# Transformer block pair on one core: order of turns, splits and copies in the attention stage, and the bank of the last chunk

## The chip, the core and the metric

The kernel runs on one core of a Trainium2 chip. Its engines are TensorE (PE, matrix products and transpositions), VectorE (DVE), ScalarE (ACT), GpSimd (POOL) and SyncE (SP); each works through its own program in order and waits on semaphores. The metric is the time of one execution on the device, in microseconds (us); lower is better. The time before is 1011.17 us, the median of three runs.

## The reference, cut to what matters

The input is 256 tokens of width 1024. A first block of two layers comes first; then the second block, whose attention is the third stage that is changed here:

```python
hn = rms_norm_2(x, ln_g[l])
proj = jnp.einsum('bsd,dc->bsc', hn, w_in[l])
(qa, ka, va, ga, qb, kb, vb, gb, qc, kc, vc, gc, gate_logits) = jnp.split(proj, SPLIT_POINTS, axis=-1)
o_a = moba_attention(...)        # 8 heads of 64
o_b = dilated_attention(...)     # 3 x 8 heads of 64
o_c = swa_sink_attention(...)    # 8 heads of 64, keys and values of only 2 shared heads
branches = jnp.stack([o_a * silu(ga), o_b * silu(gb), o_c * silu(gc)], axis=2)
br = jnp.einsum('bsiw,iwd->bsid', branches, w_branch[l])
merged = jnp.sum(sigmoid(gate_logits) * br, axis=2)
x = x + jnp.einsum('bsd,de->bse', merged, w_out[l])
```

Queries and keys are normalised per head before the logits; the logits get a bias by distance, then a softmax.

## The kernel before, in words

**Weights and matmuls.** The 256 tokens are two blocks of 128. Weights come from memory in units of at most 2048 columns per partition (1 MB) into a ring of three slots. ACT rounds a unit to `w_hi` (`round_unit`, L1022), DVE takes the rest `w_lo` (`split_unit`, L1662), and PE makes three matmuls in place of one, `hi*hi`, `hi*lo` and `lo*hi` (L434 to L436). SP loads the next unit into a slot when the slot's split is done (L262). ACT and DVE work two units ahead of PE: `slot_step` (L1034, L1669) rounds or splits the unit that PE needs two steps later. A step is one unit of four 128-row pieces on both blocks, 24 matmuls; a chunk of up to 512 output columns is two steps, and goes to the banks `acc[0]` and `acc[1]`, one for each block.

**The five attention groups.** The heads of the third stage run in five groups of eight heads, as four pairs each. The first three are passes of a loop (full attention and two dilations), the fourth is the third dilation, the fifth the window with shared keys. While a group's attention runs, PE also projects the next three chunks, so a group is six steps s = 0 to 5. In PE's program (`project_and_attend`, L661 to L689), for pair t:

- turns (`turn_pair`, L567; `turn_tokens`, L573): four transpositions of queries and keys into one bank, `qkT_ps`, which is `acc[2]`; pair 0 in the middle of step 0 (between the two blocks), pair 1 before step 1, pair 2 in its middle, pair 3 at its end. Each waits until ACT has copied the pair before out of the bank;
- logits of pair s at the end of step s, then the turn of the probabilities of pair s-1 (`turn_probs`, L600), then the values of pair s-2 (`values`, L620);
- turn of the outputs of pair s-3 (`turn_outputs`, L635) in the middle of steps 3, 4 and 5, and of pair 3 after step 5. It waits until ACT has copied these outputs and until DVE has read those of the pair before out of the bank.

ACT (`project_and_attend`, L1183) does in a step, in this order: copy of outputs, `slot_step`, what is left of the chunk before, copies of turned pairs (`copy_pair`, L1121, two activations each), the exponentials of pair s-1 and the copy of the probabilities of pair s-2, at step 1 the copy of pair 3, and then the copy of a chunk that has ended. DVE (L1910) does `slot_step`, the maxima of pair s (`maxima`, L1750), its half of the copy of probabilities, the reading of outputs (`token_outputs`, L1817) and the group's own extras. A step number in `late` moves `slot_step` behind the step's attention work; on DVE it still stands ahead of the reading of outputs. Before, `late` is (4,) in the fourth group and empty in the others.

**Between the fourth and the fifth group.** The last chunk of the fourth group is 256 wide: keys and values of the two shared window heads. ACT copies and squares it (`window_kv`, L1477); DVE sums the squares (L2155), makes the scale and writes the scaled keys to all eight heads in two instructions, one for each block (`window_keys`, L2150, L2161). The second of them releases the first turn of the fifth group through `qk_ready`.

**The end.** Six gate chunks and six branch chunks alternate in `acc[0:2]`; ACT copies the last one to `branch_out` (L1640). PE then waits for all reads, `pe.wait_ge(acc_read, n.chunk * 2)`, and starts the output projection, which uses all four `acc` banks.

Of the kernel before, what the change touches and what calls it, by code (L numbers as in the profile page):

```python
# [24 lines left out]
P = 128  # L25
TB = 2
# [44 lines left out]
def build_program(nc, x, w_in0, w_uq, w_ukv, w_out0, w_qkv, rel_band, w_out1, w_gate, w_up, w_down, g_final,  # L71
# [7 lines left out]
    with ctx:  # L79
# [85 lines left out]
        qk_banks = [qkT_ps[:, :]] + acc_banks  # L165
# [5 lines left out]
        def probs_of(kind, t):  # L171
            return mla_probs[t] if kind == "mla" else logit[:, t % 3, :, :]

# [31 lines left out]
        qk_ready = sem("qk_ready")  # L205
        qkT_done = sem("qkT_done")
# [205 lines left out]
        def _(pe):  # L412
# [154 lines left out]
            def turn_pair(kind, t, banks=(0,)):  # L567

                qkT_ps = qk_banks[banks[t % len(banks)]]
                since(pe, qkT_read, n.turn - min(t, len(banks) - 1))  # L570
                turn_tokens(t, qkT_ps)

# [88 lines left out]
            def project_and_attend(widths, kind, qk, copied, outs=head_outs, closing=None):  # L661
# [5 lines left out]
                for width in widths:  # L667
                    for k0 in (0, 4):
                        def between(blk, s=s):
                            if s == 0 and blk == 1:  # L670
                                group_ready(qk, copied)
                                pe.wait_ge(out_read, pair0)
                                turn_pair(kind, 0)
                            if s == 1:
                                turn_pair(kind, 1 + blk)
                            if s >= 3 and blk == 1:
                                turn_outputs(s - 3, pair0, turn0, outs)
                            if s == 5 and blk == 1:
                                if closing:
                                    closing()  # L680
                                attention_step(kind, 5, pair0, turn0)
                        chunk_unit(uT_hi, uT_lo, range(k0, k0 + 4), width, k0 == 0, k0 == 4, between)
                        if s == 1:
                            turn_pair(kind, 3)
                        if s < 5:
                            attention_step(kind, s, pair0, turn0)
                        s += 1
# [288 lines left out]
            for i in range(3):  # L976
                if i:
                    turn_branch(i, turn_banks)
                for half in range(2):
# [6 lines left out]
                    chunk(oT_hi, oT_lo, 4, 512, x_kt=4 * (i % 2))  # L986
# [15 lines left out]
        def _(act):  # L1002
# [118 lines left out]
            def copy_pair(kind, t, pair0, banks=(0,)):  # L1121

                qkT_ps = qk_banks[banks[t % len(banks)]]
                act.wait_ge(qkT_done, n.turn + 1)
                if kind == "last":
                    activation(qkT[:, t, 0:S], qkT_ps[:, 0:S], ACT.Copy, scale=g_now[:, 0:1])
                    activation(qkT[:, t, S:2 * S], qkT_ps[:, S:2 * S], ACT.Copy,
                               scale=g_now[:, 1:2]).then_inc(qkT_read, 1)
                else:
                    activation(qkT[:, t, :], qkT_ps[:, :], ACT.Copy).then_inc(qkT_read, 1)  # L1130
# [1203 lines left out]
```

## Time and profile before

| | |
|---|---|
| time, median of 3 runs (lowest to highest) | 1011.17 us (1009.79 to 1012.47) |
| time of the profiled execution | 1009.69 us |
| its span, first to last instruction | 1007.9 us |
| PE busy | 984.0 us, 98% |
| DVE busy | 629.4 us, 62% |
| ACT busy | 594.7 us, 59% |
| DMA | 170.26 MB, 169 GB/s over the span |
| mean granted clock of TensorE | 0.998 |

Busy is the time in which at least one instruction of the engine was in work. Rows of the timeline give start, duration, engine, line, operation, target <- sources, shapes and count, and in brackets the idle time before and what ended it. Matmuls overlap, so their pace is read from the distance of starts and not from their durations.

### The profile page before, as it was taken

Reading aid. Unit: us, or ns where it says so; the run is one execution under the profiler, and the core shown is the slowest. Engines: PE = TensorE matmul, PEld = TensorE weight load, DVE = VectorE, ACT = ScalarE, POOL = GpSimd, SP = SyncE. Lnnn points to the kernel's source line nnn. Section 1 sums busy time; section 2 is a strip of 40 time slices with the busy share of each in tenths; the row PEclk is TensorE's granted clock in tenths of the full one; section 3 lists DMA queues with packets and bytes.
Section 4 is the critical chain, followed back from the end, with each engine's and each line's share of the span. In section 5 each row is a group of like instructions: output and inputs, shape, how many; then the busy total and the mean of one; then the engine's idle time right before and its main releaser. Section 6 shows DMA issues by size and latency. Waiting matters only on the chain.

```text
span 1007.9 us, 13330 instructions
## 1 busy us (share of the span) xinstructions
PE 984.0 (98%) x4920; PEld 791.8 (79%) x4920; DVE 629.4 (62%) x782; ACT 594.7 (59%) x929; POOL 12.2 (1%) x22
## 2 busy tenths in 40 slices
PE   6999899999999999999999999999999998999998
PEld 5888688888887777788888887877777777778877
DVE  5676675555556765665555556866666666776654
ACT  6776564444445655465454545766767676867571
POOL 1000000000000000000000000000000000000000
PEclk9999999999999999999999999999999999999999
DMA  8536247756563543457757654646434334336551
GB/s 272 177 114 204 84 137 239 247 169 206 168 206 128 180 155 125 127 168 254 227 188 227 231 185 132 207 163 199 132 125 134 116 126 135 118 124 209 197 179 42
DMA packets 106041, 170.26 MB, mean 169 GB/s; under 512 B 3988, under 2 KB 65302, under 8 KB 106000
## 3 DMA queue, kind: packets, MB, share of 16 engines
q1 hardware_dynamic: 103360, 161.23, 48.6%
q0 software_dynamic: 2304, 8.37, 2.6%
q8 instruction: 27, 0.44, 0.2%
q10 hardware_dynamic: 336, 0.10, 0.0%
q14 instruction: 14, 0.11, 0.0%
HBM read 168.58 MB, written 1.11 MB: 168 GB/s over the span
## 4 chain that ended last, share of the span: by engine, by line
PE 91%; ACT 4%; DVE 4%; issue 1%; DMA 0%; ACTq 0%; DVEq 0%
PE acc L434 13%; PE acc L436 12%; PE acc L435 12%; PE acc L485 11%; PE pair_ps L436 7%; PE pair_ps L434 7%; PE pair_ps L435 7%; PE acc L536 3%; PE acc L713 3%; PE acc L630 2%; PE turn_ps L609 2%; PE pair_ps L597 1%; PE acc L577 1%; PE pair_ps L596 1%; PE turn_ps L503 1%
## 5 line engine op out<-in xcount | busy, mean ns | idle before, releaser
L1666 DVE TENSOR_TENSOR w_lo<-w_raw,w_hi 128x2048 fp32r<-128x2048 f32 (+2 forms) x155 | 345.5, 2231 | 133.4 <-ACT w_hi L1027 133.0
L1027 ACT ACTIVATE w_hi<-w_raw 128x2048 fp32r<-128x2048 f32 (+2 forms) x155 | 288.4, 1863 | 78.3 <-PE acc L436 35.5
L434 PE MATMUL acc<-w_hi,uT_hi 128*128 128x512 f32 (+3 forms) x552 | 221.4, 401 | 3.5 <-DVE w_lo L2093 3.0
L436 PE MATMUL acc<-w_hi,uT_lo 128*128 128x512 f32 (+3 forms) x552 | 212.5, 385 | 0.0
L435 PE MATMUL acc<-w_lo,uT_hi 128*128 128x512 f32 (+3 forms) x552 | 211.9, 384 | 0.0
L434 PEld LDWEIGHTS acc<-w_hi,uT_hi 128*128 128x128 f32 x552 | 104.0, 188 | 30.9 <-issue 9.0
L434 PE MATMUL pair_ps<-w_hi,uT_hi 128*128 128x512 f32 x320 | 126.5, 395 | 0.0
L436 PE MATMUL pair_ps<-w_hi,uT_lo 128*128 128x512 f32 x320 | 124.8, 390 | 0.0
L435 PE MATMUL pair_ps<-w_lo,uT_hi 128*128 128x512 f32 x320 | 124.6, 389 | 0.0
L436 PEld LDWEIGHTS acc<-w_hi,uT_lo 128*128 128x128 f32 x552 | 104.0, 188 | 21.2
L435 PEld LDWEIGHTS acc<-w_lo,uT_hi 128*128 128x128 f32 x552 | 104.3, 189 | 17.4
L436 PEld LDWEIGHTS pair_ps<-w_hi,uT_lo 128*128 128x128 f32 x320 | 60.0, 188 | 12.8
L435 PEld LDWEIGHTS pair_ps<-w_lo,uT_hi 128*128 128x128 f32 x320 | 60.2, 188 | 12.0
L434 PEld LDWEIGHTS pair_ps<-w_hi,uT_hi 128*128 128x128 f32 x320 | 60.1, 188 | 11.9
L1150 ACT ACTIVATE logit<-logit,negmax 128x128 f32<-128x128 f32 (+1 forms) x124 | 54.7, 445 | 13.7 <-DVE negmax L1763 13.7
L1509 ACT ACTIVATE oT_hi<-turn_ps 128x512 fp32r<-128x512 f32 x22 | 13.2, 599 | 76.1 <-PE turn_ps L503 76.1
L1758 DVE SCALAR_TENSOR_TENSOR logit<-pair_ps,bias 128x256 f32<-128x256 f32 (+1 forms) x56 | 28.6, 552 | 44.6 <-PE pair_ps L597 43.6
L485 PE MATMUL acc<-w_hi,oT_hi 128*128 128x512 f32 x176 | 54.4, 390 | 0.7 <-ACT logit L1109 0.7
L2053 DVE SCALAR_TENSOR_TENSOR qkv<-pair_ps,norms,qkv 128x256 f32<-128x256 f32 x40 | 17.5, 479 | 59.8 <-ACT qkv L1505 59.8
L485 PE MATMUL acc<-w_lo,oT_hi 128*128 128x512 f32 x176 | 54.2, 389 | 0.0
L485 PE MATMUL acc<-w_hi,oT_lo 128*128 128x512 f32 x176 | 54.2, 389 | 0.0
L1109 ACT ACTIVATE qkv<-acc,norms 128x512 f32<-128x512 f32 x44 | 29.6, 685 | 36.1 <-PE acc L436 36.1
(230 smaller groups left out, 1230.9 us busy)
## 6 DMA issues: line engine op xcount, KB each, us to landing
w_raw<-in_w_in SPq DMA_DIRECT2D x46, 1024.0 KB
w_raw<-in_w_gate SPq DMA_DIRECT2D x44, 512.0 KB
w_raw<-in_w_up SPq DMA_DIRECT2D x44, 512.0 KB
w_raw<-in_w_down SPq DMA_DIRECT2D x22, 1024.0 KB
w_raw<-in_w_out SPq DMA_DIRECT2D x12, 1024.0 KB
w_raw<-in_w_qkv SPq DMA_DIRECT2D x16, 512.0 KB
w_raw<-in_w_branch SPq DMA_DIRECT2D x6, 1024.0 KB
bias<-rel_rows POOLq DMA_DIRECT2D x5, 1024.0 KB, 7.9
```

The costliest lines, as they stand in the source:

```text
L434: mm(o, xh, wh[:, k, :], start=first and k == 0, stop=False)
L435: mm(o, xh, wl[:, k, :], start=False, stop=False)
L436: done = mm(o, xl, wh[:, k, :], start=False, stop=last and k == len(kts) - 1)
L485: done = mm(acc[2 * blk + half][:, :], xp, wp[:, k, 512 * half:512 * half + 512], start=first and k == 0 and i == 0, stop=last and k == 1 ...
L536: done = mm(acc[2 * blk + half][:, :], xp, wp[:, k, 512 * half:512 * half + 512], start=False, stop=k == 1 and j == 2)
L609: done = transpose(turn_ps[:, j, P * i:P * i + P], probs_of(kind, t)[:, j, P * i:P * i + P], ident[:, :])
L713: done = mm(acc[2 * blk + half][:, :], xp, wp[:, k, 512 * half:512 * half + 512], start=first and k == 0 and j == 0, stop=last and k == 1 ...
L1027: activation(w_hi[:, slot, 0:width], w_raw[:, slot, 0:width], ACT.Copy).then_inc(hi_done, 1)
L1109: done = activation(dst, src, func, scale=scale)
L1150: done = activation(pr[:, j, cols], pr[:, j, cols], ACT.Exp, bias=negmax8[:, blk, head], accum_out=total8[:, blk, head])
L1666: v.tensor_tensor(w_lo[:, slot, 0:width], w_raw[:, slot, 0:width], w_hi[:, slot, 0:width].bitcast(f32), ALU.subtract).then_inc(lo_done, 1)
L1758: done = v.scalar_tensor_tensor(pr[:, :, cols][:, :, ::-1], pair_ps[:, :, cols][:, :, ::-1], scale, bias_of(t, mask_cols), ALU.mult, ALU.add)
```

## The change

It has five parts. (1) In a group, PE turns the pairs 0, 1 and 2 in one go in the middle of step 0, into three banks (`qkT_ps` and the two halves of `turn_ps`), and pair 3 at the end of step 0, behind a wait for the copy of pair 0. ACT copies pairs 0, 1, 2 in step 0 and pair 3 in step 1 ahead of the exponentials. Before the logits of step 1 PE waits until three pairs are copied. (2) The turns of the outputs of pairs 0 and 1 move from the middle of steps 3 and 4 to their ends, behind the values; that of pair 2 moves behind the values in the middle of step 5. (3) `late` becomes (4, 5) in the fourth group and (2,) in the fifth, and DVE's reading of outputs comes before a late `slot_step`. (4) The window keys are written in three pieces, the first for the first pair alone, both blocks at once; it releases the first turn, and a new semaphore, `keys_spread`, releases the turns of pairs 1 and 2, which in this group follow step 0. (5) The last branch chunk goes to `acc[2:4]`.

```diff
-        qk_banks = [qkT_ps[:, :]] + acc_banks
+        qk_banks = [qkT_ps[:, :]] + turn_banks + [qkT_ps[:, :]]
...
+        def branch_banks(i, half):
+            return acc[2:4] if (i, half) == (2, 1) else acc[0:2]
...
-            def turn_pair(kind, t, banks=(0,)):
-
-                qkT_ps = qk_banks[banks[t % len(banks)]]
-                since(pe, qkT_read, n.turn - min(t, len(banks) - 1))
-                turn_tokens(t, qkT_ps)
...
                             if s == 0 and blk == 1:
                                 group_ready(qk, copied)
                                 pe.wait_ge(out_read, pair0)
-                                turn_pair(kind, 0)
-                            if s == 1:
-                                turn_pair(kind, 1 + blk)
-                            if s >= 3 and blk == 1:
-                                turn_outputs(s - 3, pair0, turn0, outs)
+                                for t in range(1 if n.window else 3):
+                                    turn_tokens(t, qk_banks[t])
                             if s == 5 and blk == 1:
                                 if closing:
                                     closing()
                                 attention_step(kind, 5, pair0, turn0)
+                                turn_outputs(2, pair0, turn0, outs)
                         chunk_unit(uT_hi, uT_lo, range(k0, k0 + 4), width, k0 == 0, k0 == 4, between)
+                        if s == 0 and n.window:
+                            pe.wait_ge(keys_spread, 1)
+                            for t in (1, 2):
+                                turn_tokens(t, qk_banks[t])
+                        if s == 0:
+                            pe.wait_ge(qkT_read, turn0 + 1)
+                            turn_tokens(3, qk_banks[3])
                         if s == 1:
-                            turn_pair(kind, 3)
+                            pe.wait_ge(qkT_read, turn0 + 3)
                         if s < 5:
                             attention_step(kind, s, pair0, turn0)
+                        if s in (3, 4):
+                            turn_outputs(s - 3, pair0, turn0, outs)
...
-                    chunk(oT_hi, oT_lo, 4, 512, x_kt=4 * (i % 2))
+                    chunk(oT_hi, oT_lo, 4, 512, x_kt=4 * (i % 2), banks=branch_banks(i, half))
...
-                    for t in ((0,), (1, 2))[s] if s < 2 else ():
-                        copy_pair(kind, t, pair0)
+                    for t in ((0, 1, 2), (3,))[s] if s < 2 else ():
+                        copy_pair(t)
                     attention_step(kind, s, pair0, head0)
                     if s in late:
                         slot_step(prefetch[s])
-                    if s == 1:
-                        copy_pair(kind, 3, pair0)
...
-                               prefetch=(UNIT, UNIT, 1024, 1024, UNIT, UNIT), late=(4,))
+                               prefetch=(UNIT, UNIT, 1024, 1024, UNIT, UNIT), late=(4, 5))
             project_and_attend([swish_gate(1), swish_gate(2), lambda: gate_exponentials(0)], "last", 32, 8, outs=window_outs,
-                               after={3: factors(0, 1, 4), 5: lambda: split_banks(oT_hi, 0, 4, pair_banks)})
+                               after={3: factors(0, 1, 4), 5: lambda: split_banks(oT_hi, 0, 4, pair_banks)}, late=(2,))
...
-                    copy_chunk(lambda blk: [(branch_out[:, blk, :], acc[blk][:, :], ACT.Copy, 1.0)])
+                    banks = branch_banks(i, half)
+                    copy_chunk(lambda blk: [(branch_out[:, blk, :], banks[blk][:, :], ACT.Copy, 1.0)])
...
                     attention_step(kind, s, n.pair, head0, bias_of)
+                    if 3 <= s:
+                        token_outputs(s - 3, n.pair, head0)
                     if s in late:
                         slot_step(prefetch[s])
-                    if 3 <= s:
-                        token_outputs(s - 3, n.pair, head0)
...
-                for blk in range(TB):
-                    done = v.tensor_tensor(
-                        qkv[:, 1, blk, :].rearrange("p (g r d) -> p g r d", g=2, r=4),
-                        window_kvs[:, blk, 0:P].rearrange("p (g d) -> p g d", g=2).unsqueeze(2).broadcast_to([P, 2, 4, HD]),
-                        stat[:, 2, 2 * blk:2 * blk + 2].unsqueeze(2).unsqueeze(3).broadcast_to([P, 2, 4, HD]), ALU.mult)
-                done.then_inc(qk_ready, 1)
+                scale = stat[:, 2, 0:4].rearrange("p (b n) -> p b n", b=TB)
+
+                def spread(group, r0, count):
+                    c0 = HD * (4 * group + r0)
+                    return v.tensor_tensor(
+                        qkv[:, 1, :, c0:c0 + HD * count].rearrange("p b (r d) -> p b r d", d=HD),
+                        window_kvs[:, :, HD * group:HD * group + HD].unsqueeze(2).broadcast_to([P, TB, count, HD]),
+                        scale[:, :, group:group + 1].unsqueeze(3).broadcast_to([P, TB, count, HD]), ALU.mult)
+                spread(0, 0, 2).then_inc(qk_ready, 1)
+                spread(0, 2, 2)
+                spread(1, 0, 4).then_inc(keys_spread, 1)
```

DVE's two calls get the same `late` as ACT's.

## Rows read from the trace of the kernel before

**Rows 1.** The page: busy time of each engine, and what the DMA moved.

```profile
PE 984.0 (98%) x4920; PEld 791.8 (79%) x4920; DVE 629.4 (62%) x782; ACT 594.7 (59%) x929; POOL 12.2 (1%) x22
...
DMA packets 106041, 170.26 MB, mean 169 GB/s; under 512 B 3988, under 2 KB 65302, under 8 KB 106000
```

**Rows 2.** Waits, PE: us in total, times, longest.

```profile
PE acc L434 <- DVE w_lo L2093: 3.0, 1, 3.0
...
PE acc L485 <- ACT logit L1109: 0.7, 1, 0.7
```

**Rows 3.** Timeline, PE, end of the fourth group and first half of the fifth.

```profile
835.71 0.28 PE L436 MATMUL acc<-w_hi,uT_lo 128*128 128x256 f32 x1
837.17 0.41 PE L641 MATMUL acc<-ident,heads 128*128 128x128 f32 x2 [1.18 <-issue]
...
842.61 0.39 PE L436 MATMUL acc<-w_hi,uT_lo 128*128 128x512 f32 x1
844.11 0.66 PE L577 MATMUL acc<-ident,qkv 128*128 128x128 f32 x4 [1.12 <-DVE qkv L2161]
...
856.18 0.88 PE L609 MATMUL turn_ps<-ident,logit 128*128 128x128 f32 x6
857.56 0.47 PE L434 MATMUL acc<-w_hi,uT_hi 128*128 128x512 f32 x1 [0.51 <-ACT bias L1109]
...
864.79 0.84 PE L609 MATMUL turn_ps<-ident,logit 128*128 128x128 f32 x6 [0.66 <-ACT logit L1150]
```

**Rows 4.** Timeline, PE, first pass of the loop: four turns, then six, between matmuls.

```profile
660.27 0.60 PE L577 MATMUL acc<-ident,qkv 128*128 128x128 f32 x4
...
660.93 0.40 PE L435 MATMUL acc<-w_lo,uT_hi 128*128 128x512 f32 x1
661.17 0.40 PE L436 MATMUL acc<-w_hi,uT_lo 128*128 128x512 f32 x1
...
672.29 0.88 PE L609 MATMUL turn_ps<-ident,logit 128*128 128x128 f32 x6
673.01 0.50 PE L434 MATMUL acc<-w_hi,uT_hi 128*128 128x512 f32 x1
```

**Rows 5.** Timeline, DVE, end of the fourth group: splits, readings of outputs, window keys.

```profile
834.44 2.29 DVE L1666 TENSOR_TENSOR w_lo<-w_raw,w_hi 128x2048 fp32r<-128x2048 f32 x1 [0.29 <-ACT w_hi L1027]
836.65 0.42 DVE L1821 TENSOR_SCALAR heads<-acc 128x256 f32<-128x256 f32 x1
836.99 2.28 DVE L1666 TENSOR_TENSOR w_lo<-w_raw,w_hi 128x2048 fp32r<-128x2048 f32 x1
...
840.26 0.42 DVE L1821 TENSOR_SCALAR heads<-acc 128x256 f32<-128x256 f32 x1 [0.66 <-PE acc L641]
...
841.08 0.42 DVE L2155 TENSOR_REDUCE stat<-square 128x4 f32<-128x256 f32 x1 [0.24 <-ACT square L1484]
...
842.76 1.29 DVE L2161 TENSOR_TENSOR qkv<-bias,stat 128x512 f32<-128x512 f32 x2
```

**Rows 6.** Timeline, ACT, both groups: probabilities, pair 3, rounding, exponentials.

```profile
836.49 0.48 ACT L1156 ACTIVATE prT<-turn_ps 128x384 f32<-128x384 f32 x1
...
855.42 0.47 ACT L1126 ACTIVATE qkT<-acc,g_now 128x256 f32<-128x256 f32 x1 [0.62 <-PE acc L577]
...
860.67 1.90 ACT L1027 ACTIVATE w_hi<-w_raw 128x2048 fp32r<-128x2048 f32 x1
862.47 0.39 ACT L1150 ACTIVATE logit<-logit,negmax 128x128 f32<-128x128 f32 x1
```

**Rows 7.** Windows: eight turns in a row of the fifth group; PEclk is the granted clock.

```profile
core 0: us, PE busy (x) PEld busy (x) DVE busy (x) ACT busy (x) POOL busy (x), PEclk, DMA share, GB/s
885.20:886.30 1.10, 1.10 (x13) 0.93 (x12) 1.07 (x2) 0.40 (x1) 0.00 (x0) 1.00 0.00 0
```

**Rows 8.** Waits of SP's DMA queue, 800 to 930 us: total, times, longest.

```profile
SPq L266 <- DVE w_lo L1666: 121.6, 18, 12.9
```

**Rows 9.** Timeline, PE, start of the program: first and last of six such matmuls.

```profile
11.71 0.63 PE L435 MATMUL acc<-w_lo,uT_hi 128*128 128x512 f32 x1
...
13.84 0.63 PE L434 MATMUL acc<-w_hi,uT_hi 128*128 128x512 f32 x1
```

More of the change, by code:

```diff
@@ L205, in build_program @@
         qk_ready = sem("qk_ready")
+        keys_spread = sem("keys_spread")
         qkT_done = sem("qkT_done")
@@ L1118, in plain, with copy_pair @@
                 return lambda blk: [(dst(blk), banks[blk][:, 0:width], ACT.Copy, scale_of(blk))]
-            def copy_pair(kind, t, pair0, banks=(0,)):
-                qkT_ps = qk_banks[banks[t % len(banks)]]
+            def copy_pair(t):
+                bank = qk_banks[t]
                 act.wait_ge(qkT_done, n.turn + 1)
[L1125 to L1130, printed above, removed]
+                activation(qkT[:, t, 0:S], bank[:, 0:S], ACT.Copy, scale=g_now[:, 0:1])
+                activation(qkT[:, t, S:2 * S], bank[:, S:2 * S], ACT.Copy,
+                           scale=g_now[:, 1:2]).then_inc(qkT_read, 1)
                 n.turn = n.turn + 1
@@ L2159, in window_keys @@
                 sharpen(*[stat[:, i, 0:4] for i in range(4)], HD)
-                for blk in range(TB):
-                    done = v.tensor_tensor(
-                        qkv[:, 1, blk, :].rearrange("p (g r d) -> p g r d", g=2, r=4),
-                        window_kvs[:, blk, 0:P].rearrange("p (g d) -> p g d", g=2).unsqueeze(2).broadcast_to([P, 2, 4, HD]),
-                        stat[:, 2, 2 * blk:2 * blk + 2].unsqueeze(2).unsqueeze(3).broadcast_to([P, 2, 4, HD]), ALU.mult)
-                done.then_inc(qk_ready, 1)
+                scale = stat[:, 2, 0:4].rearrange("p (b n) -> p b n", b=TB)
[8 more added lines that the diff above has]
+                spread(1, 0, 4).then_inc(keys_spread, 1)
                 n.qk = n.qk + 1
             project_and_attend(6, "last", 24, table(3), {1: head_sums, 3: lambda: swish_gate(0), 5: window_keys},
-                               prefetch=(UNIT, UNIT, 1024, 1024, UNIT, UNIT), after_unit={2: head_norm(0)}, late=(4,))
+                               prefetch=(UNIT, UNIT, 1024, 1024, UNIT, UNIT), after_unit={2: head_norm(0)}, late=(4, 5))
             def nm(group):
@@ L2241, in _ @@
                 0: full_over_total, 1: lambda: swish_gate(1), 2: first_gate, 3: lambda: swish_gate(2),
-                4: dilation_weights}, closing={5: lambda: split_banks(oT_hi, oT_lo, 0, 4, pair_banks)})
+                4: dilation_weights}, closing={5: lambda: split_banks(oT_hi, oT_lo, 0, 4, pair_banks)}, late=(2,))
             for i in range(3):
```

## The prediction

> **What bounds the kernel now.** I read the page first. The matrix engine (PE) has work in flight for 98% of the span [rows 1], so only its idle time and its time per instruction can give anything. The list of waits comes next. Its PE part is short, and its largest entry, 3.0 us, lies at the start of the program, outside the change [rows 2]. Then I went through PE's timeline over the five attention groups of the third stage. In the three groups of the loop no gap is listed. The gaps lie in the last two groups [rows 3]:
>
> - fourth group, middle of step 5: the stream stops after the matmul at 835.71, and the next instruction, the turn of the outputs of pair 2, starts at 837.17. Without a wait it would start about 0.12 later (a 256-wide matmul's pace, half of the 0.23 that a 512-wide one takes [rows 4]), so 1.34 us are lost.
> - fifth group, first turn of pair 0: 842.61 to 844.11, 1.27 us lost beyond one matmul.
> - fifth group, start of the second chunk: 856.18 to 857.56, for six turns that take 0.11 each [rows 4]: 1.38 - 0.66 = 0.72 lost.
> - fifth group, probabilities of pair 1: 0.66 idle, put down to ACT's exponentials.
>
> Who releases them is read from the other two engines. The first gap is called "issue", but the turn waits until DVE has read the outputs of pair 1 (836.65), and DVE does that only after a split of weights begun at 834.44 and 2.29 long [rows 5]. Right behind it the values of pair 3 would wait anyway: ACT copies their probabilities at 836.49, behind a rounding of weights [rows 6]. The second gap ends with DVE's two instructions from 842.76, which write the window keys to all heads. They end a chain whose sum starts at 841.08, after the reading of pair 3's outputs at 840.26 [rows 5]. The third ends with ACT's copies of the chunk, which stand behind the copy of pair 3 at 855.42; the fourth with exponentials at 862.47, which stand behind the rounding at 860.67 [rows 6].
>
> **The change, part by part.** Times are in us; gains are negative.
>
> *Turns in one go.* Four turns take 0.43: from 660.27 to the second matmul behind them at 660.93 is 0.66, less one matmul of 0.23 (660.93 to 661.17 is 0.24) [rows 4]. Twelve in a row then take 1.3, as three times four do now. Entering and leaving the turns shows no price of its own in these rows, so the move costs 0. The nearest rows bound it at 0.1 either way per group, five groups: -0.5 to +0.5. The same holds for the turns of outputs that move behind the values. What hides the copies: pair 0 must be read by ACT (two copies of 0.47 [rows 6]) while PE runs the second half of step 0, 12 matmuls of 0.23 or 2.7. Pairs 1 and 2 have all of step 1, 24 matmuls or 5.5. If that cover were gone, PE would pay up to 0.85 per pair. Logits of pair 0 come 1.3 later in the step (12 turns stand in front of them, none today), and DVE's maxima and ACT's exponentials of pair 0 move with them. They are needed only behind step 1.
>
> *Clock.* Eight turns in a row ran at a granted clock of 1.00, the 2.4 GHz level [rows 7]. The Trainium skill (TensorE: Matmul & The Clock Gate, Part 4: PE-mode transpose) says that turns on this engine do not count as busy time for its clock; by that rule the longer run of turns could let the clock fall, and the sum would lose some 6 us. By the row it loses 0, which I take.
>
> *Copy of pair 3 first.* It leaves the place between the exponentials and the chunk's copies, so ACT reads the chunk as soon as PE ends it. Fifth group: -0.72. In the loop the same spot shows 672.29 to 673.01 for six turns, 0.72 against 0.66 or less [rows 4]; I take -0.1 for each of four groups, -0.4 (between 0 and -0.7). What is late next there: nothing that I find before the end of the chunk.
>
> *Split of step 2 behind the exponentials, fifth group.* The rounding at 860.67 takes 1.90 [rows 6] and stands in front of exponentials for which PE waits 0.66 [rows 3]. With the two exchanged, and the chunk's copies earlier as well, the gap closes: -0.66 (bounds 0 and -0.66). The rounding and DVE's split come some 4 later. PE needs that unit two steps on, over 10 away; were that cover gone, PE would wait for what is missing.
>
> *Outputs before splits, fourth group.* DVE reads pair 1's outputs before the split of 2.29, and ACT copies pair 3's probabilities before the rounding of 1.91: both releasers of the first gap come forward by over 1.3, and the gap closes: -1.34. What is queued behind: DVE's split of step 4 now waits for PE's turn and for that read, 0.42, so it ends about 837.2. The read of pair 2 follows at 837.2, and the split of step 5, which began at 836.99 [rows 5], now begins about 837.5 and ends 839.8. Pair 3's outputs, turned by PE at about 838.5, are read only then, at 839.7, not 840.26, and the sum of the keys starts at about 840.25, not 841.08: 0.83 earlier, though PE is 1.34 earlier.
>
> *Keys as a piece.* The two instructions from 842.76 take 1.29 for 1024 elements per partition [rows 5]. The first piece has 256. A DVE read of 256 elements takes 0.42 (836.65) [rows 5]; a quarter of 1.29 would be 0.32, one of today's two 0.65. I take 0.42, by the row of its own size: 0.87 earlier. The first turn then starts at 844.11 - 0.83 - 0.87 = 842.4, and PE reaches it at 842.84 - 1.34 = 841.5. A gap of 0.9 stays of 1.27: -0.37 (bounds: 0 with a late chain, -1.27 if it closes). The two other pieces, about 1.1 together, are done by 843.6; PE asks for them some 2.7 after the first turn.
>
> *Loads.* The splits that come later also free their slots later, by at most some 4, and SP's loads wait for exactly these splits [rows 8]. A unit of 1 MB at the mean rate of 169 GB/s [rows 1] takes about 6.2. It is rounded three steps after the split that freed the slot, some 16 or more even with short steps, so this stays hidden. GpSimd's queue has no part in these stretches.
>
> *Last chunk in other banks.* PE still waits for both reads of every chunk before the output projection, which is the 0.7 in the list [rows 2]; only the bank number changes. 0.
>
> **Sum.** 0.72 + 0.4 + 0.66 + 1.34 + 0.37 = 3.5 off. The profiled execution took 1009.69, its span 1007.9; the sum makes that 1006.2 and 1004.4. Its time is 1.5 below the median of the three runs (1011.17) and 0.1 below their fastest, so as base for the median I take the mean of all four times, 1010.8: **1007.3**.
>
> **Rivals.** A measurement of this kernel tells about 0.3% from no change, 3.0 us here: faster means below 1008.1.
>
> *The logits' delay takes the freed places.* In the fifth group the logits of pair 0 stand behind 12 turns, 1.3 later in the step; if ACT's exponentials of pair 0 then end so late that the chunk is again read late, the gaps of 0.72 and 0.66 return in another form. For it: ACT is a single queue, and each step of that chain stood in a gap today. Against it: pair 2's copy and pair 3's copy leave that very stretch. 3.5 - 1.4 = 2.1 off: 1008.7. Chance 0.22.
>
> *More closes than I count.* The remaining 0.9 at the first turn and the 0.7 ahead of the output projection (if the other banks release it after all) vanish: 5.1 off, 1005.7. Chance 0.12.
>
> *The clock falls behind the long run of turns.* At the start of the program matmuls ran at the lower level, 1.2 GHz: six records of 0.63, 0.43 apart, against 0.23 later [rows 9]. Before them PE had waited 3.0 [rows 2]. If twelve turns alone bring such a spell, each group loses at least 6 x 0.2 = 1.2; five groups 6.0, so 2.5 slower than before: 1013.3. It decides from three groups on. Against it: eight turns at 1.00 [rows 7], with matmuls directly before and behind. Chance 0.06. The page named above is the rule for this case; the trace does not bear it out for eight turns, and shows no twelve.
>
> *The change doesn't do what it says.* For the banks of the last chunk this is my forecast (0). For the rest the waits that are named do stand in the code that moves.
>
> **How the numbers follow.** Forecast 0.60, at 1007.3 with about 1 us of scatter either way, as the four times show. Of it some four fifths lie below 1008.1; with nearly all of the second rival and a quarter of the first this makes 0.63 faster. The rest of the forecast and most of the first rival make 0.29 for no difference; the clock, with a little for a wait that I have not seen, 0.08 slower. The range takes in the second rival with some scatter, and the first with more, since single runs of one kernel lie up to 2.8 apart: 1004.3 to 1010.3.
>
> **What would show it.** In the new profile: no wait in the fourth group's step 5; the first turn of the fifth group still after an idle time of about 0.9, ended by DVE's first piece; no idle time at the second chunk and none before the probabilities of pair 1 there; each pass of the loop shorter by about 0.1; the wait of 0.7 ahead of the output projection unchanged; granted clock 1.00 behind the runs of turns. Wrong would be a new wait of PE for ACT's copies behind step 0 or 1, for weights (w_lo) in steps 1 or 4 of the fifth group, or for the gated outputs that DVE splits at the end of the fifth group: its reads of outputs now wait for turns that come later in each step.

## The result and the profile after

| | before | after |
|---|---|---|
| time, median of 4 runs (lowest to highest) | 1010.48 us (1009.79 to 1012.47) | 1005.19 us (1005.08 to 1007.22) |
| time of the profiled execution | 1009.69 us | 1005.24 us |
| its span | 1007.9 us | 1003.5 us |

The ratio is 0.9947 (95% interval 0.9932 to 0.9961): faster, by 0.5%. The forecast was 1007.3 with a range of 1004.3 to 1010.3. Whole times of one kernel scatter by up to three us, in part because of a spell in the first layers that this change does not touch (last section). So from here on I compare what can be read to a hundredth: starts in PE's timeline. **The stretch** is the distance from the last weight matmul ahead of the first turns (before 660.03, after 660.30) to the last weight matmul of the program (before 1004.37, after 999.92). To the nanosecond it is 4.71 us shorter, where the prediction's sum was 3.5.

PE's line on the page, after:

```profile
PE 982.2 (98%) x4920; PEld 792.1 (79%) x4920; DVE 629.8 (63%) x783; ACT 595.1 (59%) x929; POOL 12.2 (1%) x22
```

Against [rows 1] PE's busy time fell by 1.8 us with the same 4920 instructions: part of the gain is not in any listed wait.

A pass of the loop is read from the first weight matmul behind the first turns of a pass. PE's timeline before:

```profile
707.13 0.47 PE L434 MATMUL acc<-w_hi,uT_hi 128*128 128x512 f32 x1
...
753.64 0.47 PE L434 MATMUL acc<-w_hi,uT_hi 128*128 128x512 f32 x1
```

and PE's timeline after, over the whole third stage (L438 to L440 are the three weight matmuls, L575 the turns of queries and keys, L607 those of probabilities, L628 the values, L639 the turns of outputs):

```profile
660.53 0.60 PE L575 MATMUL acc<-ident,qkv 128*128 128x128 f32 x4
...
661.76 0.48 PE L438 MATMUL acc<-w_hi,uT_hi 128*128 128x512 f32 x1
...
680.54 0.87 PE L628 MATMUL acc<-prT,qkv 128*64 128x256 f32 x8
...
681.35 0.50 PE L438 MATMUL acc<-w_hi,uT_hi 128*128 128x512 f32 x1
681.68 0.39 PE L439 MATMUL acc<-w_lo,uT_hi 128*128 128x512 f32 x1
...
688.68 0.87 PE L628 MATMUL acc<-prT,qkv 128*64 128x256 f32 x8
689.48 0.44 PE L639 MATMUL acc<-ident,heads 128*128 128x128 f32 x2
...
689.99 0.39 PE L439 MATMUL acc<-w_lo,uT_hi 128*128 128x512 f32 x1
...
707.96 0.48 PE L438 MATMUL acc<-w_hi,uT_hi 128*128 128x512 f32 x1
...
754.12 0.48 PE L438 MATMUL acc<-w_hi,uT_hi 128*128 128x512 f32 x1
...
834.69 0.28 PE L440 MATMUL acc<-w_hi,uT_lo 128*128 128x256 f32 x1
834.90 0.87 PE L628 MATMUL acc<-prT,qkv 128*64 128x256 f32 x8
...
841.36 0.66 PE L575 MATMUL acc<-ident,qkv 128*128 128x128 f32 x4 [0.80 <-DVE qkv L2165]
...
853.39 0.87 PE L607 MATMUL turn_ps<-ident,logit 128*128 128x128 f32 x6
854.02 0.47 PE L438 MATMUL acc<-w_hi,uT_hi 128*128 128x512 f32 x1
...
860.55 0.88 PE L607 MATMUL turn_ps<-ident,logit 128*128 128x128 f32 x6
...
976.29 0.39 PE L440 MATMUL acc<-w_hi,oT_lo 128*128 128x512 f32 x1
977.37 0.73 PE L489 MATMUL acc<-w_hi,oT_hi 128*128 128x512 f32 x2 [0.69 <-ACT logit L1114]
```

The reader should see four things. First, against [rows 3]: the gap in step 5 of the fourth group is gone (the values follow at 834.90 on the matmul at 834.69, with no idle time), the one at the second chunk of the fifth group is gone (six turns from 853.39 to 854.02, 0.63), the one ahead of the probabilities (860.55) is gone, and 0.80 is left at the first turn. Second, the wait ahead of the output projection is still 0.69, as in [rows 2]. Third, twelve turns in a row take 1.23 from 660.53 to the next matmul. Fourth, a pass of the loop went from 753.64 - 707.13 = 46.51 to 754.12 - 707.96 = 46.16 (46.15 unrounded), 0.35 less, though no wait was ever listed there.

Where the 4.71 us lie, each from differences of matmul starts, beside the prediction's term:

| stretch | predicted | measured |
|---|---|---|
| three passes of the loop | 0.3 | 1.01 |
| fourth group up to the middle of step 5 | 0.1 | 0.28 |
| the gap in step 5 and the rest of that step | 1.34 | 1.41 |
| first turn of the fifth group | 0.37 | 0.33 |
| fifth group, up to the probabilities of pair 1 (second chunk) | 0.72 | 0.76 |
| rest of the fifth group (exponentials, outputs) | 0.66 | 0.88 |
| behind it | 0 | 0.04 |

DVE's timeline after, at the end of the fourth group, answers to [rows 5]:

```profile
833.58 0.42 DVE L1822 TENSOR_SCALAR heads<-acc 128x256 f32<-128x256 f32 x1 [0.61 <-PE acc L639]
833.91 2.28 DVE L1667 TENSOR_TENSOR w_lo<-w_raw,w_hi 128x2048 fp32r<-128x2048 f32 x1
836.18 0.42 DVE L1822 TENSOR_SCALAR heads<-acc 128x256 f32<-128x256 f32 x1
836.52 2.28 DVE L1667 TENSOR_TENSOR w_lo<-w_raw,w_hi 128x2048 fp32r<-128x2048 f32 x1
838.72 0.42 DVE L1822 TENSOR_SCALAR heads<-acc 128x256 f32<-128x256 f32 x1
...
839.20 0.42 DVE L2156 TENSOR_REDUCE stat<-square 128x4 f32<-128x256 f32 x1
...
840.88 1.36 DVE L2165 TENSOR_TENSOR qkv<-bias,stat 128x256 f32<-128x256 f32 x3
```

From 833.58 to the sum at 839.20 DVE has not one pause: reads and splits alternate as predicted, and the first turn waits for the length of this queue. ACT's timeline after, fifth group, answers to [rows 6]:

```profile
848.49 0.49 ACT L1130 ACTIVATE qkT<-acc,g_now 128x256 f32<-128x256 f32 x1
...
850.96 0.70 ACT L1114 ACTIVATE square<-acc,norms 128x512 f32<-128x512 f32 x1
...
855.99 0.39 ACT L1152 ACTIVATE logit<-logit,negmax 128x128 f32<-128x128 f32 x1
...
858.12 1.90 ACT L1032 ACTIVATE w_hi<-w_raw 128x2048 fp32r<-128x2048 f32 x1
```

Pair 3 (848.49) now goes ahead of the chunk's copies (850.96), and the exponentials of pair 1 (855.99) go ahead of the rounding (858.12). Granted clock after, windows in the first layers and over the twelve turns (third number from the right):

```profile
115.00:118.00 3.00, 3.00 (x14) 2.21 (x16) 3.00 (x5) 0.00 (x0) 0.00 (x0) 1.00 0.94 296
...
660.50:661.80 1.30, 1.30 (x14) 1.26 (x12) 0.87 (x1) 1.02 (x3) 0.00 (x0) 1.00 0.95 369
```

So the signs that the prediction named are all there but one: each pass is shorter by 0.35, not by 0.1. What this leaves to find out is which part of the change made which of these gains.

### The profile page after: what moved, and what is told of

It reads as the page before. It is cut to its first block, busy times and chain, and to the rows that moved or that the text cites. A ratio compares the mean times of both kernels' runs of the same rounds, so it can differ in the third digit from the quotient of the medians.

```text
span 1003.5 us, 13324 instructions
## 1 busy us (share of the span) xinstructions
PE 982.2 (98%) x4920; PEld 792.1 (79%) x4920; DVE 629.8 (63%) x783; ACT 595.1 (59%) x929; POOL 12.2 (1%) x22
## 4 chain that ended last, share of the span: by engine, by line
PE 91%; DVE 4%; ACT 3%; issue 1%; DMA 0%; ACTq 0%; DVEq 0%
PE acc L438 13%; PE acc L440 12%; PE acc L439 12%; PE acc L489 11%; PE pair_ps L440 7%; PE pair_ps L438 7%; PE pair_ps L439 7%; PE acc L540 3%; PE acc L718 3%; PE turn_ps L607 2%; PE acc L628 2%; PE pair_ps L595 2%; DVE w_lo L1667 1%; PE pair_ps L594 1%; PE turn_ps L507 1%
## 5 line engine op out<-in xcount | busy, mean ns | idle before, releaser
L438 PE MATMUL acc<-w_hi,uT_hi 128*128 128x512 f32 (+3 forms) x552 | 219.6, 398 | 2.8 <-DVE w_lo L2094 2.8
L440 PE MATMUL acc<-w_hi,uT_lo 128*128 128x512 f32 (+3 forms) x552 | 212.4, 385 | 0.0
L438 PEld LDWEIGHTS acc<-w_hi,uT_hi 128*128 128x128 f32 x552 | 104.1, 189 | 29.2 <-issue 7.6
L438 PE MATMUL pair_ps<-w_hi,uT_hi 128*128 128x512 f32 x320 | 126.5, 395 | 0.0
L440 PE MATMUL pair_ps<-w_hi,uT_lo 128*128 128x512 f32 x320 | 124.8, 390 | 0.0
L440 PEld LDWEIGHTS acc<-w_hi,uT_lo 128*128 128x128 f32 x552 | 104.1, 189 | 21.0
L440 PEld LDWEIGHTS pair_ps<-w_hi,uT_lo 128*128 128x128 f32 x320 | 60.1, 188 | 12.8
L438 PEld LDWEIGHTS pair_ps<-w_hi,uT_hi 128*128 128x128 f32 x320 | 60.1, 188 | 11.9
```

Source lines behind the costliest of these rows:

```text
L438: mm(o, xh, wh[:, k, :], start=first and k == 0, stop=False)
L440: done = mm(o, xl, wh[:, k, :], start=False, stop=last and k == len(kts) - 1)
```

## The experiments

Unless said otherwise each is the changed kernel with one edit, and its stretch is compared with that of the changed kernel. Runs can be shifted against one another by up to 3.1 us by what happens before 660 us, so starts are compared as distances within a run.

### The late splits undone

```diff
-                               prefetch=(UNIT, UNIT, 1024, 1024, UNIT, UNIT), late=(4, 5))
+                               prefetch=(UNIT, UNIT, 1024, 1024, UNIT, UNIT), late=(4,))
...
-                               after={3: factors(0, 1, 4), 5: lambda: split_banks(oT_hi, 0, 4, pair_banks)}, late=(2,))
+                               after={3: factors(0, 1, 4), 5: lambda: split_banks(oT_hi, 0, 4, pair_banks)})
...
+                    if s in late:
+                        slot_step(prefetch[s])
                     if 3 <= s:
                         token_outputs(s - 3, n.pair, head0)
-                    if s in late:
-                        slot_step(prefetch[s])
```

DVE's two calls get the same `late` as ACT's.

> The changed kernel with its third part undone: the late steps are (4,) and none again, and DVE reads outputs behind a late split. Theory (each closed gap belongs to the late splits): the fourth group's step 5 stands still again for about 1.3 us ahead of the turn of outputs, and in the fifth group PE waits about 0.7 for the exponentials of pair 0 or 1; the passes of the loop stay at 46.15 us; span 1.4 to 2.0 us above the changed kernel. Rival (the turns of outputs moved behind the values close the step 5 gap by themselves): only the 0.7 returns, span +0.7.

Measured: 1007.65 us median, ratio to before 0.9957 (0.9943 to 0.9971). The stretch is 0.37 longer, not 1.4 to 2.0. PE's timeline of this run:

```profile
835.82 0.87 PE L628 MATMUL acc<-prT,qkv 128*64 128x256 f32 x8 [0.86 <-ACT prT L1158]
...
841.28 0.39 PE L440 MATMUL acc<-w_hi,uT_lo 128*128 128x512 f32 x1
841.72 0.66 PE L575 MATMUL acc<-ident,qkv 128*128 128x128 f32 x4
...
860.93 0.88 PE L607 MATMUL turn_ps<-ident,logit 128*128 128x128 f32 x6
```

and DVE's writing of the keys in it:

```profile
841.24 1.36 DVE L2165 TENSOR_TENSOR qkv<-bias,stat 128x256 f32<-128x256 f32 x3
```

The gap in step 5 does return (0.86), now ahead of the values and ended by ACT's copy of probabilities, but the wait at the first turn shrinks from 0.80 to about 0.2 (841.28 to 841.72, less a pace of 0.23): the writing of the keys begins at 841.24, only 0.36 later than the 840.88 of the changed kernel (the two runs are 0.01 apart at 660 us), and that is all that is lost. And in the fifth group nothing returns: no idle time at 860.93. Both theories fall: the late split of step 2 gains nothing there, and the 1.34 was not a gain of the late splits by themselves.

### The keys in two instructions

```diff
-                spread(0, 0, 2).then_inc(qk_ready, 1)
-                spread(0, 2, 2)
-                spread(1, 0, 4).then_inc(keys_spread, 1)
+                spread(0, 0, 4)
+                spread(1, 0, 4).then_inc(qk_ready, 1)
```

PE's wait for `keys_spread` goes with it.

> The changed kernel with its fourth part undone: the window keys are written in two instructions, one for each group of heads, and the second releases all turns of the fifth group. Theory (the piece of 256 took 0.42, two pieces of 512 take 1.3): the first turn of the fifth group waits 0.8 to 0.9 us longer, idle 1.6 to 1.7 in place of 0.80, and nothing behind it catches up: span +0.85. Rival (the first turn is set by the chain ahead, the sum of the keys, and the rest of the delay is absorbed by the eight turns that no longer have a wait of their own): span +0.4 or less.

Measured: 1007.91 us, ratio 0.9964 (0.9950 to 0.9977); the stretch is 0.85 longer. PE's first turn of the fifth group:

```profile
842.12 0.66 PE L575 MATMUL acc<-ident,qkv 128*128 128x128 f32 x4 [1.67 <-DVE qkv L2164]
```

The idle time is 1.67 in place of 0.80, and nothing behind it catches up. The piece is worth the 0.87 that the prediction gave it (0.85 in the stretch).

### The turns of outputs in the middle of the steps

```diff
+                            if s >= 3 and blk == 1:
+                                turn_outputs(s - 3, pair0, turn0, outs)
...
-                                turn_outputs(2, pair0, turn0, outs)
...
-                        if s in (3, 4):
-                            turn_outputs(s - 3, pair0, turn0, outs)
```

> The changed kernel with its second part undone: the turns of the outputs of pairs 0, 1 and 2 stand in the middle of steps 3, 4 and 5 again. Theory A (a pause stands behind the small fp32 matmuls of logits and values before the next weight matmul, and turns put there fill it, so that their move behind the values is a gain of its own): each pass of the loop is 0.17 to 0.22 us longer, 46.32 to 46.37 in place of 46.15, and the span about 0.9 longer over five groups. Theory B (the prediction's: a turn costs the same wherever it stands): passes stay at 46.15, span within 0.1.

Measured: 1007.93 us, ratio 0.9963 (0.9948 to 0.9977). A pass takes 46.46 us, 0.31 more; the stretch is 0.77 longer (the wait at the first turn gives some of it back: 0.29 is left of its 0.80). The turn in the middle of step 3, PE's timeline of this run:

```profile
685.40 0.39 PE L440 MATMUL acc<-w_hi,uT_lo 128*128 128x512 f32 x1
685.64 0.38 PE L639 MATMUL acc<-ident,heads 128*128 128x128 f32 x2
...
686.09 0.39 PE L439 MATMUL acc<-w_lo,uT_hi 128*128 128x512 f32 x1
```

Between weight matmuls the two turns stretch two paces of 0.23 to 685.40 to 686.09, 0.69: they cost 0.23. Behind values, in the timeline after, it is 1.31 from 688.68 to 689.99 with two turns and 1.14 from 680.54 to 681.68 without: they cost 0.17. Theory A holds in kind, but its 0.17 to 0.22 a pass was too small and its 0.9 in all too large; the prediction's zero is refuted.

### Two more turns, in the middle or at the end of step 2

Two kernels with the same addition (first four groups), the first in the middle of step 2, the second behind the values of pair 0:

```diff
+    if s == 2 and blk == 1 and not n.window:
+        pe.wait_ge(qkT_read, turn0 + 4)
+        for i in range(2):
+            transpose(qk_banks[0][:, P * i:P * i + P], ident[:, :], ident[:, :])
```

```diff
+    if s == 2 and not n.window:
+        pe.wait_ge(qkT_read, turn0 + 4)
+        for i in range(2):
+            transpose(qk_banks[0][:, P * i:P * i + P], ident[:, :], ident[:, :])
```

> The changed kernel with two more transpositions (of the unit matrix, into a bank that is free then, read by nobody) in the middle of step 2 of the first four groups, between two weight matmuls. Nothing is left out. Both theories: 0.22 to 0.24 us for each pass of the loop, 46.38 in place of 46.15. This is the reference for the next run.

> The same two further transpositions, but at the end of step 2, behind the values of pair 0 and ahead of the next weight matmul. Theory A (behind the values a weight matmul starts late in any case, and turns put there fill a part of that pause): 0.14 to 0.18 us for each pass, 46.29 to 46.33. Theory B (the prediction's: a turn costs the same wherever it stands): 0.22 to 0.24, as in the run before.

Measured: 1006.22 and 1007.43 us (ratios 0.9954, 0.9937 to 0.9971, and 0.9966, 0.9952 to 0.9980). A pass by PE's timeline, in the middle:

```profile
708.29 0.48 PE L438 MATMUL acc<-w_hi,uT_hi 128*128 128x512 f32 x1
...
754.69 0.48 PE L438 MATMUL acc<-w_hi,uT_hi 128*128 128x512 f32 x1
```

at the end:

```profile
709.63 0.48 PE L438 MATMUL acc<-w_hi,uT_hi 128*128 128x512 f32 x1
...
755.96 0.48 PE L438 MATMUL acc<-w_hi,uT_hi 128*128 128x512 f32 x1
```

46.40 and 46.33 against 46.15: the same two turns cost 0.25 between weight matmuls and 0.18 behind values. So the place has a price, 0.07 for each two turns. Three pairs of turns moved in a pass, which makes 0.2 of the 0.31 if each is worth this much (the third, in step 5, stood between a weight matmul and values, which neither of the two kernels tests; the starts there give 0.05); the other 0.1 is spread over many starts, and stays open.

### Many more turns in a row

```diff
+                                for t in () if n.window else (0, 1, 2, 0, 1, 2):
+                                    for i in range(4):
+                                        transpose(qk_banks[t][:, P * i:P * i + P],
+                                                  qkv[:, i // 2, i % 2, P * t:P * t + P], ident[:, :])
```

> The changed kernel with 24 more transpositions in each of the first four groups, ahead of the twelve of the first three pairs: the same turns into the same banks, twice over, so 36 in a row; the twelve that count overwrite them, and nothing is left out. Theory (turns cost their 0.109 us each and the clock stays up): each of four groups 2.6 us longer, loop passes about 48.8, span +10.5, granted clock 1.00 in the stretch of turns and behind it. Rival (turns do not hold the clock, which falls behind a long run of them): behind the 36 turns matmuls of 512 columns come 0.43 apart for a while, granted clock below 1.00 there, and each group is at least 1.2 longer than that: span +15 or more.

Measured: 1017.03 us, ratio 1.0054 (1.0038 to 1.0070). Each of the four groups is 2.62 longer, which is 24 times 0.109, the stretch 10.45. Windows over the 36 turns and behind them:

```profile
660.70:664.20 3.50, 3.50 (x34) 3.50 (x33) 2.29 (x1) 0.60 (x3) 0.00 (x0) 1.00 0.32 123
664.20:668.00 3.80, 3.80 (x25) 3.08 (x25) 0.00 (x0) 2.46 (x6) 0.00 (x0) 1.00 0.81 276
```

The granted clock is 1.00, the 2.4 GHz level, in both. The rival of the falling clock is refuted for runs up to 36. The Trainium skill (TensorE: Matmul & The Clock Gate, Part 4: PE-mode transpose) says that such turns do not count as busy time for the clock in the way of other matmuls; by that rule the clock could have been at risk here, and in this trace it stays at 1.00 over 3.5 us of turns. Longer runs are not shown.

### The turns alone

The kernel before with the first part of the change alone, so without the late splits, the outputs behind values, the keys in three pieces (two are written, one for each shared head) and the other banks; the diff shows the first part:

```diff
-                                turn_pair(kind, 0)
+                                for t in range(1 if n.window else 3):
+                                    turn_tokens(t, qk_banks[t])
...
-                    if s == 1:
-                        copy_pair(kind, 3, pair0)
```

> The kernel before with the first part of the change alone: the turns of three pairs in one go, pair 3 at the end of step 0, its copy ahead of the exponentials. Theory (by the run with the outputs back in the middle of the steps, where a pass took 0.31 us longer): a pass of the loop takes 46.46 us, only 0.05 less than the 46.51 before; in the fifth group the idle time ahead of the second chunk (0.51) and that ahead of the probabilities of pair 1 (0.66) are both gone, without any late split; the gap of 1.34 in step 5 of the fourth group and the wait of 1.12 at the first turn stay. Span about 1.6 below before. Rival (the prediction's: the late split of step 2 closes the second of these gaps): 0.66 stays idle, span about 1.0 below before.

Measured: 1008.92 us, ratio 0.9984 (0.9973 to 0.9996). The stretch is 1.77 below before, a pass 46.46. PE's timeline of this run:

```profile
838.51 0.41 PE L639 MATMUL acc<-ident,heads 128*128 128x128 f32 x2 [1.19 <-issue]
...
845.46 0.66 PE L575 MATMUL acc<-ident,qkv 128*128 128x128 f32 x4 [1.12 <-DVE qkv L2163]
...
858.14 0.47 PE L438 MATMUL acc<-w_hi,uT_hi 128*128 128x512 f32 x1
...
864.66 0.88 PE L607 MATMUL turn_ps<-ident,logit 128*128 128x128 f32 x6
```

and ACT's:

```profile
861.92 0.38 ACT L1150 ACTIVATE logit<-logit,negmax 128x128 f32<-128x128 f32 x1
```

Both gaps of the fifth group are gone (no idle time at 858.14 and 864.66), with the rounding (860.11, 1.90 long) still ahead of the exponentials: they begin at 861.92, in time for the turns at 864.66. ACT begins to read the chunk 3.07 ahead of PE's second chunk (855.07, 858.14); in the kernel before it was 1.41 ahead (856.15, 857.56). The theory holds. The two waits around the fourth group's end stay as they were.

### Two idle times that were left

First, ahead of the output projection: the last chunk has banks of its own since the change, but PE still waited for its reads.

```diff
-            pe.wait_ge(acc_read, n.chunk * 2)
+            pe.wait_ge(acc_read, n.chunk * 2 - 2)
...
-            proj_unit((4, 5), True, False)
+            proj_half((4, 5), 0, True, False)
+            pe.wait_ge(acc_read, n.chunk * 2)
+            proj_half((4, 5), 1, True, False)
```

> The changed kernel with one more change: ahead of the output projection PE waits for the reads of all chunks but the last, runs the first half of the unit on block 0, waits for the last chunk's reads, and runs the second half, so that the other banks of the last chunk can serve. Theory (the 0.69 us of idle time there is the wait for ACT's copies of the last chunk and nothing else): it goes, span 0.6 to 0.7 below the changed kernel. Rival (the output projection also needs something else that is just as late, its splits or its weights): the idle time stays under another releaser, span within 0.2.

Measured: 1005.84 us, ratio 0.9952 (0.9935 to 0.9968); the stretch is 0.96 shorter. PE's timeline at this place:

```profile
978.17 0.61 PE L489 MATMUL acc<-w_hi,oT_hi 128*128 128x512 f32 x2
```

No idle time is left. More than the 0.69 is gained, since the bracket counts from the end of the matmul before. By starts the wait costs 0.85: 976.29 to 977.37 is 1.08, less a pace of 0.23. The first two matmuls behind it also last 0.73 in the changed kernel against 0.61 here, which gives the other 0.1.

Second, at the first turn of the fifth group: DVE's late step 5 goes behind the window keys (on DVE only; `behind` is true in the fourth group).

```diff
-                    if s in late:
+                    if s in late and not (s == 5 and behind):
                         slot_step(prefetch[s])
...
+                    if s == 5 and behind:
+                        slot_step(prefetch[s])
```

> The changed kernel with DVE's order at the end of the fourth group changed: reading of the outputs of pair 3, sum, scale and window keys come before the split of step 5 and not behind it. Theory (the first turn of the fifth group waits for the length of DVE's queue, in which this split of 2.28 us stands in front of the keys; what is left then is ACT's square of the chunk, done at about 838.6): the sum of squares starts at about 838.65 in place of 839.20, and the idle time of the first turn falls from 0.80 to about 0.25 us; span 0.5 lower. Rival (the split that comes later is needed sooner than I think, by the rounding and loads behind it or by PE in step 1 of the fifth group): a wait for weights of 0.5 or more appears there and the span stays.

Measured: 1006.75 us, ratio 0.9964 (0.9952 to 0.9977); the stretch is 0.59 shorter. PE's first turn and, behind it, DVE's sum of squares:

```profile
842.53 0.66 PE L575 MATMUL acc<-ident,qkv 128*128 128x128 f32 x4 [0.24 <-DVE qkv L2167]
```

```profile
840.38 0.42 DVE L2158 TENSOR_REDUCE stat<-square 128x4 f32<-128x256 f32 x1 [0.23 <-ACT square L1484]
```

0.24 is left of 0.80, and the sum now waits for ACT's square of the chunk: DVE's queue was the bound, as the first experiment had it. No wait for weights appears.

Both together, and then once more, with the changed kernel again:

> The changed kernel with both further changes, the split wait ahead of the output projection and the keys ahead of the split. Theory (the two idle times lie 100 us apart and have nothing to do with one another): their gains add up, 1.1 to 1.3 us below the changed kernel. Rival (the later splits push the chain that sets the end, so that one gain eats the other): no more than 0.7.

> The changed kernel itself once more, timed beside the version with both further changes. Theory (in some executions matmuls of the first layers run at half the clock from 115 us on, for about 3 us, which costs about 1.5 us, outside the change and by chance): the span is 1003.5, or 1.4 to 1.8 above that if the profiled execution has this spell; from 660 us to the end 4.7 us less than before in either case. Rival (the spell comes with the change): before has it in no profile and this kernel in every one.

> The version with the split wait ahead of the output projection and the keys ahead of the split, once more. Theory: from 660 us to the end 6.2 us less than before, that is 1.5 less than the changed kernel; its median 1.0 to 2.0 below that of the changed kernel in this call. Rival (whole times drown this): the medians lie within 0.5.

Measured, both edits: 1006.09 us, ratio 0.9948 (0.9934 to 0.9962), and the second time 1006.36, ratio 0.9944 (0.9930 to 0.9959); the changed kernel beside the latter 1005.80, ratio 0.9950 (0.9938 to 0.9962). The stretch of the version with both edits is 6.25 below before in both profiles, 1.54 below the changed kernel, which is 0.96 + 0.59: the gains add up, and are larger than expected because the wait ahead of the output projection was worth more than its bracket. The medians do not show it: that of both edits lies 0.56 above the changed kernel's, not 1.0 to 2.0 below, and just outside the rival's 0.5 too. The lowest times do, 1003.46 against 1004.87. The changed kernel's own stretch repeats to 0.03, and the time of its second profile is 2.2 us above that of the first: 0.8 of it arises in the first 16 us of the program, 1.4 in the spell told in the last section.

## Why the prediction was right, and where its steps were not

**Right in sign, cautious in size.** The stretch gained 4.71 where the sum said 3.5. The four gaps that were read from the timeline were rightly sized: 1.41 for 1.34, 0.33 for 0.37, 0.76 for 0.72, and of the last 0.88 about 0.70 is the gap for which 0.66 stood. The median came out 2.1 below the forecast, and only 1.2 of that is the stretch; the rest lies in whole times that scatter by more (the second median of the same kernel is 1005.80), so how far inside the range it fell is in part luck.

**The step that failed: "Entering and leaving the turns shows no price of its own in these rows, so the move costs 0. [...] The same holds for the turns of outputs that move behind the values."** For turns between weight matmuls the rows did show that. For the outputs the rows read were of the wrong place: behind values the stream of weight matmuls starts slowly anyway (681.35 to 681.68 is 0.33, against a pace of 0.23), and turns put there cost 0.18 for two and not 0.25. This part of the change, put at 0, gives 0.31 a pass and 0.77 in all. The 0.1 per group that stood for the earlier copy of pair 3 was too large: with the turns alone a pass gains 0.05.

**Two terms had the right size under the wrong part.** "With the two exchanged, and the chunk's copies earlier as well, the gap closes." It closes without the exchange (the turns alone), and undoing the exchange loses nothing. The first part by itself closes it: pair 3's copy no longer stands ahead of the chunk's copies, and the chunk is read sooner (3.07 in place of 1.41 ahead of PE's second chunk, with the turns alone), so the rounding and the exponentials behind it come sooner too. And the 1.34 of the fourth group is not the late splits' own: without them only 0.37 is lost, since DVE's queue then ends just 0.36 later and the first turn waits less. The prediction treated the step 5 gap and the first turn as two terms, and did follow the one into the other ("0.83 earlier, though PE is 1.34 earlier"); but that the two together are bounded by one queue of DVE, so that a gain at the first shows up as a wait at the second, it used for the sum only and not for the credit of each part.

**The parts do not add up.** Undoing one part loses 0.77 (outputs), 0.37 (late splits) or 0.85 (keys); the turns alone bring 1.77. That is about 3.8 of 4.71. The rest, about 0.9, belongs to the end of the fourth group, where several parts relieve the same queue; no run splits it up.

**Costed at nothing, and rightly:** the copies that ACT makes under step 0 and step 1, the delayed logits (no idle time at either place of the first rival), the loads, and the other banks for the last chunk, which do nothing until the wait is split. The first rival did not happen; the second did in part (there was an excess, but not by its mechanism: the first turn's 0.80 and the 0.69 stayed); the clock stayed up.

## What to carry to other kernels

In these runs two turns cost 0.25 between two wide matmuls and 0.18 behind the small ones of the values: try the place where the wide stream is broken already, and price it by starts there. Where one queue feeds two waits in a row, a gain at the first is worth only what the queue's end moves, so credit a part by undoing it alone. Where whole times scatter by more than the effect, compare the starts of the same matmuls on both sides of the change.

## What was not expected of the hardware

In some executions the first layers have a spell at a lower clock, far from anything changed. PE waits 2.46 us for DVE there, and the matmuls behind the wait run either at a granted clock of 1.00, the 2.4 GHz level (the window 115.00:118.00 of after, above), or at 0.50, the 1.2 GHz level, as in the second profile of the same changed kernel, windows:

```profile
116.00:118.50 2.50, 2.50 (x7) 1.92 (x8) 2.50 (x5) 0.00 (x0) 0.00 (x0) 0.50 0.92 274
```

The same wait (2.45 and 2.46) came before both. The spell cost this profile 1.4 us, and 2.9 in the longest case (the second profile with both edits). It was there in eight of the fourteen profiles, and not in the one of before; the changed kernel has it in one profile and not in the other, so the change does not bring it each time. A like spell from about 11 us on, at the start of the program, is in twelve of the fourteen; the two without it (the second profile of the changed kernel and the first with both edits) both have the one at 115 us. Single times of before, with no profile, lie between 1009.57 and 1012.81, as far apart as those of the changed kernel (1004.87 to 1007.60). What decides it, and whether some of these kernels have it more often, stays open.
